# A hybrid decoder step on one core: ScalarE's and VectorE's order of work in the delta stage

## The chip, the cores and the metric

The kernel runs on one core of a Trainium2 chip. Its time is the device time of one execution in microseconds (us); several runs are given by their median. Engines carry the names of the profile: PE is TensorE (PEld its weight loads), DVE is VectorE, ACT is ScalarE, POOL is GpSimd, SP is SyncE, which here only issues transfers.

## What is computed

One layer of a decoder for 528 prompt tokens (16 learned ones and 512) and 8 sample sequences of 4 tokens, all float32. Cut to what matters:

```python
def gdn_chunk(S, q, k, v, g, beta):            # one chunk of tokens, 4 heads of 128
    G = jnp.cumsum(g, axis=-1)
    decay = jnp.exp(jnp.where(incl, G[..., :, None] - G[..., None, :], -jnp.inf))
    kb = k * beta[..., None]
    L = jnp.where(strict, jnp.einsum('bhik,bhjk->bhij', kb, k) * decay, 0.0)
    rhs = jnp.concatenate([v * beta[..., None], kb * jnp.exp(G)[..., None]], axis=-1)
    sol = lax.linalg.triangular_solve(L, rhs, left_side=True, lower=True, unit_diagonal=True)
    ...
    return S_new, o

def token_mixer(...):
    proj = xn @ w_in                           # q, k, v, z, a, b and the Conformer's input
    ...                                        # short convolution, l2norm of q and k
    S_new, o = gdn_prompt(S0f, q, k, v, g, beta) if prompt else gdn_recurrent(...)
    o = rmsnorm(o.transpose(0, 2, 1, 3), gdn_norm_w) * jax.nn.silu(z)
    c = causal_dwconv(c_ext, conf_dw_w) + conf_dw_b      # 31 taps, 512 channels
    c = jax.nn.silu(layernorm(c, conf_ln_w, conf_ln_b))
    out = jnp.concatenate([o, c], axis=-1) @ w_out
    return out, ...

h = h + token_mixer(rmsnorm(h)); h = h + peer_ffn(rmsnorm(h))   # then a last RMSNorm
```

`peer_ffn` picks 16 of 16384 one-neuron experts per head and token (8 heads) and adds their outputs up.

## The kernel before, in words

**Stages.** The span falls into the input projection, the delta stage (about 140 to 404 us: the chunks of the recurrence, the Conformer's convolution and layer norm, the last blocks of the input projection, the sample sequences), the output and query projections (404 to 530), the choice of experts, and two dense passes over all experts (to 1237 and to the end), each step of which PE computes while the next weights are split into a high and a low part.

**The delta stage.** The prompt is cut into chunks 0 (48 rows: 32 of the sample, 16 learned tokens) and 1 to 4 (128 rows each). Each engine has a generator `tile(ci)` for each chunk that yields named steps: `gb` (cumulated gates), `k` (keys transposed to rows), `khT` (normalized keys transposed back), `kk` and `kq` (products of keys, and of keys and queries), `ldT`, `v`, `p2` to `t3` (inverse of the 16-wide diagonal blocks), `n` to `nt4` and `r0` to `r3` (the solve), `wT`, `ws`, `qs`, `su`, `o1` (state and output). `ke` is ScalarE's step that scales the transposed keys into `RA` (second half) and `KE` (for chunk 0 `KEM`). Other generators run beside the chunks: `late_blocks` (20 units of the input projection, each two halves of 12 matmuls on PE and an evacuation on ScalarE), `sample_tile` (`sw0` to `sw3`, `ktm`, `su00` to `su31`), `norm_tile_conf` (layer norm: sums `ls`, squares `sq`, `lv`, root `lr`, inverse root `li`, products `lm` on VectorE, SiLU `ln` on ScalarE), `mix_tile` (`conformer`, `cl0` to `cl3`: high and low parts of the layer norm's output, `high`: high part of the first output weights, `table`, `delta`), `outs`, `roots`, `onbs` (RMSNorm of the recurrence's outputs: `oss` sums of squares, `root`, `onb`, `on`).

**What sets the order.** A table gives each step a time: `FIRST[ci]` plus `LEVEL[n]` or, for a few steps, `HEAD[n][ci]`; the other generators have tables of absolute times (`SAMPLE_AT`, `OUT_AT`, `NORM_AT`, `MIX_AT`). `side_by_side` (L507) writes out, for each engine by itself, always the generator whose next step has the lowest time. An engine then works strictly in this order; a wait of one step holds everything behind it. The same times deal out the PSUM banks: `GROUPS` is sorted by them, a step takes the next bank of the ring, and `free_bank` (L1005) makes PE wait until those that read the bank before are done. The bank of `k` is given back by VectorE's `k` and ScalarE's `ke` (L474). VectorE's `feed` (L2287) puts the 124 accumulations of the convolution (L1943, 528 columns) between the steps by the same times.

**Steps that the change touches**, before: ScalarE runs the exponentials of a chunk (L1533 to L1536, eight instructions) in step `gb`, at `HEAD["gb"]`, ahead of `ke` (L1541 and L1550) and `khT` (`take`, L1523: a copy out of PSUM). Chunk 3 alone has `khT` ahead of `ke`. VectorE's `kk` waits for the exponentials (L2086). The sums of squares of the outputs of the sample and chunks 1 and 2 are on ScalarE (L1611: four squares with an accumulated sum), those of chunks 3 and 4 on VectorE (L2168: a product of 512 columns, L2169: a reduction). The low part of the first output weights is GpSimd's (L848); it waits for ScalarE's `high`.

Of the kernel before, what the change touches and what calls it, by code (L numbers as in the profile page):

```python
# [32 lines left out]
HEADS, DH = 4, 128  # L33
# [16 lines left out]
CHUNKS = [(0, MIXED)] + [(MIXED + P * i, P) for i in range(SEQ // P)]  # L50
# [123 lines left out]
def build(nc, ins, outs, counts):  # L174
# [13 lines left out]
    with ctx:  # L188
# [229 lines left out]
        for b in range(nb):  # L418
# [4 lines left out]
        SAMPLE, TAILS, NORM, LIN, MIX = range(len(CHUNKS), len(CHUNKS) + 5)  # L423
        OUTS = (SAMPLE, 1, 2, 3, 4)
        SET = {0: 0, 1: 0, 2: 0, 3: 2, 4: 0}
        FIRST = {0: 4.2, 1: 12.5, 2: 27.9, 3: 41.3, 4: 43.6}
        HEAD = {"gb": {0: -2.4, 1: -2, 2: -2.4, 3: -1.2, 4: -1.28}, "k": {0: -1.3, 1: -0.8, 2: -0.7, 3: -0.2, 4: -0.8},
                "ke": {0: -0.9, 1: -0.1, 2: -0.3, 3: 1.05, 4: -0.4}, "su": {0: 9.1, 1: 14, 2: 14, 3: 14, 4: 14.15}}
        END_AT = 54.65

        LEVEL = {"khT": 1, "kk": 2, "kq": 2.1, "ldT": 3, "v": 3.1, "p2": 4, "pt2": 4.1,
# [5 lines left out]
        SAMPLE_AT = {"sw0": 42.4, "sw1": 42.9, "sw2": 43.7, "sw3": 44.2, "ws": 44.25, "qs": 44.3, "o1": 45.2}  # L437
        for hh in range(HEADS):
            SAMPLE_AT[f"ktm{hh}"] = 49.4 + 1.2 * hh
            SAMPLE_AT[f"su{hh}0"], SAMPLE_AT[f"su{hh}1"] = 50.2 + 1.2 * hh, 50.25 + 1.2 * hh  # L440
        OUT_AT = {"oss": {SAMPLE: 46.5, 1: 46.6, 2: 46.7, 3: 55.45, 4: 57.82},
                  "root": {SAMPLE: 46.8, 3: 56.65, 4: 58.02},
                  "onb": {SAMPLE: 48.9, 1: 50.1, 2: 51.1, 3: 56.68, 4: 58.05},
                  "on": {SAMPLE: 49.6, 1: 50.7, 2: 51.7, 3: 57.8, 4: 58.95}}
        NORM_AT = {"ls": 48.5, "lc": 48.55, "sq0": 49.3, "sq1": 49.35, "lv0": 50.3, "lv1": 50.8, "sq2": 50.85,
                   "lv2": 51.3, "sq3": 51.32, "lv3": 51.75, "lr": 51.85, "li0": 52.2, "li1": 52.45}
        for c in range(NG):
            NORM_AT[f"lm{c}"], NORM_AT[f"ln{c}"] = 52.5 + 0.2 * c, 52.6 + 0.2 * c
        MIX_AT = {"conformer": 53.8, "cl0": 54.0, "cl1": 54.2, "cl2": 54.4, "cl3": 54.6, "high": 54.8, "table": 55.65,
                  "out0a": 57.85, "out1a": 57.9, "out2a": 57.95, "delta": 57.96, "deltalow": 58, "out0b": 58.6,  # L450
                  "out1b": 58.9, "out2b": 59.2}
        TAILS_AT = {"tail0": 40.65, "tail1": 40.85, "tail2": 41.05, "tail3": 41.2}
# [888 lines left out]
        def _(act):  # L1341
            def fn(out, in_, f, *name, **kw):
                return A.op(act.activation(out, in_, f, **kw), *name)
# [167 lines left out]
            def each_head(n, out, in_, scale, ci):  # L1511

                for hh in range(HEADS):
                    fn(out(hh), in_(hh), ACT.Identity, *((n, ci) if hh == HEADS - 1 else ()), scale=scale(hh))

            def tile(ci):
                c0, c = CHUNKS[ci]
                B = SETS[SET[ci]]
                KH, KHT, KE, RA, RB, M, AT, VN = (B[n_] for n_ in ("KH", "KHT", "KE", "RA", "RB", "M", "AT", "VN"))
                if ci == 0:  # L1520
                    KE = KEM

# [8 lines left out]
                yield "gb", ci
                V.wait(act, "arg", ci)
                for hh in range(HEADS):  # L1533
                    fn(M[6][0:c, hh, 0:c], M[6][0:c, hh, 0:c], ACT.Exp, bias=row_of(GCB, c, ci, hh), scale=-1.0)
                    fn(M[5][0:c, hh, 0:c], M[5][0:c, hh, 0:c], ACT.Exp, "exp", ci, bias=row_of(NGC, c, ci, hh),
                       scale=1.0)  # L1536
                if ci == len(CHUNKS) - 2:
                    yield "khT", ci
                    take("khT", KHT[:, :, 0:c], P)
                    yield "ke", ci  # L1540
                    V.wait(act, "k", ci)  # L1541
                    if ci == 1:
                        T.wait(act, "r0b", 0)
                    if ci == 0:
                        V.wait(act, "qconv", 3 * HEADS - 1)
                    each_head(None, lambda hh: RA[0:c, hh, 1, :], of_head("k"), lambda hh: row_of(RKB, c, ci, hh), ci)
                    each_head("ke", lambda hh: KE[0:c, hh, :], of_head("k"), lambda hh: row_of(RKE, c, ci, hh), ci)
                else:
                    yield "ke", ci
                    V.wait(act, "k", ci)  # L1550
                    if ci == 1:
                        T.wait(act, "r0b", 0)
                    if ci == 0:
                        V.wait(act, "qconv", 3 * HEADS - 1)
                    each_head(None, lambda hh: RA[0:c, hh, 1, :], of_head("k"), lambda hh: row_of(RKB, c, ci, hh), ci)
                    each_head("ke", lambda hh: KE[0:c, hh, :], of_head("k"), lambda hh: row_of(RKE, c, ci, hh), ci)
# [259 lines left out]
        def _(dve):  # L1816
# [778 lines left out]
```

## Time and profile before

| | us |
|---|---|
| median of 3 runs | 1844.85 |
| lowest, highest run | 1838.57, 1849.69 |
| the profiled execution, its own time | 1842.69 |
| its span, first to last instruction | 1840.9 |
| PE busy in the span | 1777.0 (97%) |
| DVE busy | 1384.3 (75%) |
| ACT busy | 712.9 (39%) |
| POOL busy | 681.8 (37%) |
| mean granted clock of PE | 0.991 |

The profile is of one execution. Busy time is the time in which an engine executes; a timeline gives an instruction's start, its length and, in brackets, how long its engine sat idle before it and whose end ended that. PEclk is the TensorE clock that was granted, as a share of full speed. Plain float32 matmuls appear twice each (four of a step as x8), transposes and the split projections once.

### The profile page before, as it was taken

How to read it: one execution, taken by the hardware profiler on the slowest of the kernel's cores; microseconds unless marked ns; L12 is line 12 of the kernel's file. 1: busy time of each engine (PE TensorE's matmuls, PEld its weight loads, DVE VectorE, ACT ScalarE, POOL GpSimd, SP SyncE). 2: the span in 40 equal slices, each digit the busy share in tenths (PEclk: the TensorE clock that was granted, in tenths of full speed). 3: DMA queues.
4: the chain of work that ended last, by engine and by line, in shares of the span. 5: the costliest groups of instructions: out<-in, count | busy, mean ns of one | idle time of the engine just before them, and what ended most of it. 6: DMA issues, size and time to landing. Idle time of an engine off the chain costs nothing.

```text
span 1840.9 us, 29413 instructions
## 1 busy us (share of the span) xinstructions
PE 1777.0 (97%) x11497; PEld 1728.0 (94%) x11497; DVE 1384.3 (75%) x2533; ACT 712.9 (39%) x1244; POOL 681.8 (37%) x448
## 2 busy tenths in 40 slices
PE   7999987979999999999999999999999999999998
PEld 6998886879999999999999999999999999999997
DVE  4887887674899999999865665437697888887752
ACT  4546325453333334443433333333233333333332
POOL 3000000000004586777876767742353333333100
PEclk9999999999999999999999999999999999999999
DMA  7211101053313688888998989899999999999731
GB/s 215 69 47 43 36 5 49 24 150 124 118 47 111 218 275 264 295 294 311 300 322 293 308 313 318 289 378 354 338 402 374 339 347 361 342 342 355 293 118 38
DMA packets 190706, 424.33 MB, mean 231 GB/s; under 512 B 11162, under 2 KB 119222, under 8 KB 180320
## 3 DMA queue, kind: packets, MB, share of 16 engines
q1 hardware_dynamic: 153256, 287.47, 45.3%
q0 software_dynamic: 37312, 134.97, 20.8%
q8 instruction: 92, 1.51, 0.3%
q14 instruction: 46, 0.38, 0.1%
HBM read 360.76 MB, written 62.06 MB: 230 GB/s over the span
## 4 chain that ended last, share of the span: by engine, by line
PE 75%; DVE 19%; ACT 3%; issue 2%; POOL 1%; DMA 0%; SPq 0%; DVEq 0%; ACTq 0%; POOLq 0%
PE psum L1321 32%; PE psum L1300 21%; PE psum L927 9%; PE psum L1288 3%; PE psum L922 3%; DVE cT L1943 2%; DVE junk L2461 2%; PE psum L1030 2%; PE psum L1078 1%; DVE besti L2336 1%; DVE oh L2451 1%; DVE besti L2324 1%; DVE sring L2328 1%; DVE eqx L2394 1%; DVE pick L2399 1%
## 5 line engine op out<-in xcount | busy, mean ns | idle before, releaser
L1300 PE MATMUL psum<-xT,WS 128*128 128x416 f32 x3072 | 594.8, 353 | 2.8 <-POOL WS L862 2.7
L1321 PE MATMUL psum<-AR,WS 128*128 128x416 f32 x3072 | 582.1, 351 | 2.6 <-DVE AR L2532 2.6
L1321 PEld LDWEIGHTS psum<-AR,WS 128*128 128x128 f32 x3072 | 575.6, 188 | 9.0 <-DVE AR L2532 3.0
L1300 PEld LDWEIGHTS psum<-xT,WS 128*128 128x128 f32 x3072 | 572.2, 188 | 8.5 <-POOL WS L862 4.0
L862 POOL TENSOR_TENSOR WS<-RAWP,WS 128x1024 fp32r<-128x1024 f32 x128 | 310.9, 2439 | 315.6 <-ACT WS L1730 215.0
L853 POOL DMA_INDIRECT rowg<-in_expert_v,idx x128 | 182.0, 1422 | 317.6 <-DVE acc L2475 309.7
L927 PE MATMUL psum<-xT,WR 128*128 128x280 f32 (+2 forms) x1968 | 272.0, 296 | 4.7 <-DVE WR L1830 3.3
L1740 ACT ACTIVATE WS<-RAWP 128x1024 fp32r<-128x1024 f32 x128 | 135.6, 1059 | 336.2 <-PE psum L1321 325.9
L927 PEld LDWEIGHTS psum<-xT,WR 128*128 128x128 f32 x1968 | 258.1, 191 | 6.6 <-DVE WR L1830 3.6
L2525 DVE TENSOR_TENSOR WS<-RAWP,WS 128x1024 fp32r<-128x1024 f32 x128 | 156.5, 1223 | 116.2 <-ACT WS L1740 116.2
L1767 ACT ACTIVATE actA<-psum 128x416 f32<-128x416 f32 x128 | 66.3, 518 | 401.8 <-PE psum L1300 395.5
L2461 DVE CUSTOM_DVE_ANT_0 junk<-rowg,psum 128x1024 bf16<-128x1024 f32 x128 | 155.9, 1218 | 51.8 <-DMA rowg<-in_expert_u_rows,idx 43.8
L853 POOL DMA_INDIRECT rowg<-in_expert_u_rows,idx x128 | 166.0, 1297 | 37.6 <-issue 22.7
L2475 DVE SCALAR_TENSOR_TENSOR acc<-rowg,coef,acc 128x1024 f32<-128x1024 f32 x128 | 163.8, 1279 | 3.2 <-DMA rowg<-in_expert_v,idx 1.0
L2451 DVE TENSOR_TENSOR oh<-iotab,pairs 128x2048 bf16<-128x2048 bf16 x52 | 93.7, 1801 | 93.0 <-PE psum L1288 92.2
L1730 ACT ACTIVATE WS<-RAWP 128x1024 fp32r<-128x1024 f32 x128 | 134.5, 1053 | 0.0
L1943 DVE SCALAR_TENSOR_TENSOR cT<-gext,dwcols,cT 128x528 f32<-128x528 f32 x120 | 92.3, 769 | 4.2
L840 POOL MEMSET WQP<- 128x2048 f32 x1 | 1.8, 1809 | 246.9 <-PE psum L927 246.9
L2454 DVE TENSOR_TENSOR ohg<-oh,pairs 128x3072 bf16<-128x3072 bf16 x52 | 91.5, 1759 | 1.8
L2523 DVE TENSOR_TENSOR act<-act,Gt 128x416 f32<-128x416 f32 x128 | 74.9, 585 | 12.7 <-DMA act<-act_dram 9.1
L1792 ACT ACTIVATE AR<-act 128x416 fp32r<-128x416 f32 x128 | 69.0, 539 | 36.9 <-DVE act L2523 36.9
L2532 DVE TENSOR_TENSOR AR<-act,AR 128x416 fp32r<-128x416 f32 x128 | 74.9, 585 | 7.3 <-ACT AR L1792 7.3
(372 smaller groups left out, 1662.0 us busy)
## 6 DMA issues: line engine op xcount, KB each, us to landing
RAWP<-in_expert_u SPq DMA_DIRECT2D x64, 1024.0 KB
RAWP<-in_expert_v SPq DMA_DIRECT2D x64, 1024.0 KB
act_dram<-actA SPq DMA_DIRECT2D x128, 208.0 KB
gate_dram<-gblk SPq DMA_DIRECT2D x26, 1024.0 KB
act<-act_dram SPq DMA_DIRECT2D x64, 416.0 KB
Gt<-gate_dram SPq DMA_DIRECT2D x16, 1664.0 KB
RAW<-in_w_in SPq DMA_DIRECT2D x8, 1024.0 KB, 6.0
RAW<-in_w_query SPq DMA_DIRECT2D x8, 1024.0 KB, 8.0
```

The lines of the kernel that those rows point to most:

```text
L853: pool.indirect_dma_start(out=rowg[:, s_ % 4, :], out_offset=None, in_=table, in_offset=bass.IndirectOffsetOnAxis(ap=idx[:, s_ % PAIRS:s_ ...
L862: pool.tensor_tensor(ws(n)[:, 1], raw(n), ws(n)[:, 0].bitcast(F32), ALU.subtract).then_inc(u_low, 1)
L927: last = mm(bank[u % 4][:, 0:hw], W[:, pw, kt, m * P:(m + 1) * P], xT[:, px, kt, c0:c0 + hw], **go)
L1300: last = mm(bank[e % 2][:, 0:TD], ws(e)[:, pw, kt * P:(kt + 1) * P], xT[:, px, kt, TSP:TPE], start=(kt == 0 and i == 0), stop=(kt == KT - ...
L1321: last = mm(bank[dt][:, 0:TD], ws(NK + e)[:, pw, dt * P:(dt + 1) * P], AR[:, e % 4, pa, :], start=(e == 0 and i == 0), stop=(e == NK - 1 a ...
L1730: act.activation(ws(n)[:, 0], raw(n), ACT.Copy).then_inc(u_high, 1)
L1740: act.activation(ws(n)[:, 0], raw(n), ACT.Copy).then_inc(v_high, 1)
L1943: op(dve.scalar_tensor_tensor(d, x, w, d, ALU.mult, ALU.add))
L2451: chain(tt(by_two(oh[:, i]), keys_, per_token(0, 2), ALU.is_equal))
L2461: dve.tensor_tensor_reduce(junk[:], rowg[:, s_ % 4, :], xnP, 1.0, 0.0, ALU.mult, ALU.add, sdot[:, s_:s_ + 1]).then_inc(dot_done, 1)
L2475: dve.scalar_tensor_tensor(acc[:], rowg[:, s_ % 4, :], coef[:, s_:s_ + 1], acc[:], ALU.mult, ALU.add).then_inc(axpy_done, 1)
L2525: tt(ws(NK + e)[:, 1], raw(NK + e), ws(NK + e)[:, 0].bitcast(F32), ALU.subtract).then_inc(v_low, 1)
```

## The change

It does three things.

1. ScalarE's exponentials get a step of their own, `exp`, with a row of times of its own. For chunk 0 the order on ScalarE becomes `khT`, `exp`, `ke` (before: `gb`, `ke`, `khT`), at 5.2, 5.25 and 5.3 instead of 1.8, 3.3 and 5.2. For chunk 4 the step moves from 42.32 to 42.4, so that chunk 3's `ke` (42.35) comes first on ScalarE.
2. The layer norm's second inverse root, its products and its SiLU get later times (`li1` 52.45 to 52.87, `lm` 52.5 + 0.2c to 52.95 + 0.25c, `ln` 52.6 + 0.2c to 53.31 + 0.25c), the sample's `su20` and `su21` go from 52.6 and 52.65 to 52.92 and 52.94, `conformer` and `cl0` to `cl3` are moved too.
3. Chunk 3's sums of squares move from VectorE to ScalarE, to just ahead of `root`.

Nothing else is computed in another way, and no transfer is added or taken away.

By these times the orders become the following, where they differ (before, then after; the number behind the point is the chunk, S the sample):

```
ACT  unit0 gb.0 ke.0 unit1 khT.0 unit2 | unit0 unit1 khT.0 exp.0 ke.0 unit2
ACT  khT.3 gb.4 ke.3 ke.4              | khT.3 ke.3 exp.4 ke.4
ACT  n2.4 ln0 ln1 nt2.4 ktm3.S ln2 ln3 wT.3 nt4.4 | n2.4 nt2.4 ktm3.S wT.3 ln0 ln1 nt4.4 ln2 ln3
ACT  wT.4 table root.3                 | wT.4 table oss.3 root.3
PE   n2.4 su20 su21 r1a.4 r1b.4 nt2.4  | n2.4 r1a.4 r1b.4 nt2.4 su20 su21
DVE  li1 lm0 su20 su21 r1a.4 lm1 r1b.4 lm2 ktm3.S lm3 r2a.4 | r1a.4 r1b.4 li1 su20 su21 lm0 ktm3.S lm1 lm2 r2a.4 lm3
DVE  cl0 cl1 ws.3                      | cl0 ws.3 cl1
DVE  o1.3 oss.3 ws.4                   | o1.3 ws.4 oss.3
```

```diff
-        HEAD = {"gb": {0: -2.4, 1: -2, 2: -2.4, 3: -1.2, 4: -1.28}, ...
-                "ke": {0: -0.9, 1: -0.1, 2: -0.3, 3: 1.05, 4: -0.4}, ...
+        HEAD = {"gb": {0: -2.4, 1: -2, 2: -2.4, 3: -1.2, 4: -1.2},
+                "exp": {0: 1.05, 1: -2, 2: -2.4, 3: -1.2, 4: -1.2}, ...
+                "ke": {0: 1.1, 1: -0.1, 2: -0.3, 3: 1.05, 4: -0.4}, ...
+        SAMPLE_AT["su20"], SAMPLE_AT["su21"] = 52.92, 52.94
-        OUT_AT = {"oss": {SAMPLE: 46.5, 1: 46.6, 2: 46.7, 3: 55.45, 4: 57.82},
+        OUT_AT = {"oss": {SAMPLE: 46.5, 1: 46.6, 2: 46.7, 3: 56.62, 4: 57.82},
-                   "lv2": 51.3, "sq3": 51.32, "lv3": 51.75, "lr": 51.85, "li0": 52.2, "li1": 52.45}
+                   "lv2": 51.3, "sq3": 51.32, "lv3": 51.75, "lr": 51.85, "li0": 52.2, "li1": 52.87}
-            NORM_AT[f"lm{c}"], NORM_AT[f"ln{c}"] = 52.5 + 0.2 * c, 52.6 + 0.2 * c
-        MIX_AT = {"conformer": 53.8, "cl0": 54.0, "cl1": 54.2, "cl2": 54.4, "cl3": 54.6, ...
+            NORM_AT[f"lm{c}"], NORM_AT[f"ln{c}"] = 52.95 + 0.25 * c, 53.31 + 0.25 * c
+        MIX_AT = {"conformer": 54.1, "cl0": 54.2, "cl1": 54.35, "cl2": 54.5, "cl3": 54.65, ...
...
+                if ci == 0:
+                    yield "khT", ci
+                    take("khT", KHT[:, :, 0:c], P)
+                    yield "exp", ci
+                    exps()
+                    yield "ke", ci
+                    keys()
...
             def outs():
-                for i, ci in enumerate(OUTS[:-2]):
+                for i, ci in enumerate(OUTS[:-1]):
...
                     yield "oss", ci
-                    if ci in OUTS[-2:]:
+                    if ci == OUTS[-1]:
                         squares = SETS[SET[ci]]["RB"][:, :, 0, :]
```

`exps()` and `keys()` hold the instructions that stood in `gb` and `ke`, with the same waits. For chunks 1, 2 and 4 the order inside a chunk is `exp`, `ke`, `khT`, for chunk 3 `exp`, `khT`, `ke`, as before.

## Rows read from the trace of the kernel before

**Rows 1.** The page's part on the chain that ended last, by engine

```profile
PE 75%; DVE 19%; ACT 3%; issue 2%; POOL 1%; DMA 0%; SPq 0%; DVEq 0%; ACTq 0%; POOLq 0%
```

**Rows 2.** Busy time by stretch: start:end, length, each engine's busy (count), PEclk, DMA

```profile
404.00:530.00 126.00, 125.46 (x1041) 125.02 (x1039) 87.70 (x342) 44.12 (x77) 0.00 (x0) 1.00 0.33 102
...
295.00:300.00 5.00, 5.00 (x22) 4.34 (x22) 1.46 (x2) 2.17 (x8) 0.00 (x0) 0.50 0.00 0
```

**Rows 3.** The same view, the stretch in which chunk 0 starts

```profile
140.00:155.09 15.09, 11.96 (x100) 10.92 (x100) 6.61 (x14) 11.69 (x33) 0.00 (x0) 0.89 0.06 10
```

**Rows 4.** Timeline of ScalarE at chunk 0 (start, length, operation, idle before)

```profile
146.14 0.34 ACT L1343 ACTIVATE KHT<-psum 128x192 f32<-128x192 f32 x1
```

**Rows 5.** Timeline of TensorE at chunk 0

```profile
141.22 0.45 PE L1044 MATMUL psum<-ident,KH 48*128 48x48 f32 x4
...
146.53 0.88 PE L1047 MATMUL psum<-KHT 128*48 128x48 f32 x8 [3.13 <-ACT KHT L1343]
...
147.90 2.67 PE L927 MATMUL psum<-xT,WR 128*128 128x280 f32 x12
```

**Rows 6.** Timeline of ScalarE, exponentials of chunk 4 and keys of chunk 3

```profile
290.20 2.44 ACT L1343 ACTIVATE M<-M,tok 128x128 f32<-128x128 f32 x8 [3.55 <-DVE M L2082]
...
293.55 1.13 ACT L1343 ACTIVATE KE<-psum,tok 128x128 f32<-128x128 f32 x4
```

**Rows 7.** Timeline of TensorE behind them

```profile
286.84 1.96 PE L1140 MATMUL psum<-SS,WQP 128*64 128x128 f32 x16
...
294.82 1.09 PE L1042 MATMUL psum<-ident,kC 128*128 128x128 f32 x4 [6.03 <-ACT KE L1343]
...
295.84 3.68 PE L1140 MATMUL psum<-SS,WQP 128*64 128x128 f32 x16
...
305.33 0.66 PE L1053 MATMUL psum<-ident,M 128*128 128x128 f32 x4
```

**Rows 8.** Busy time of the same stretch

```profile
290.20:305.44 15.24, 10.62 (x69) 9.70 (x70) 6.45 (x10) 6.65 (x24) 0.00 (x0) 0.78 0.26 68
```

**Rows 9.** The view of tile SS: its loads, time from issue to landing

```profile
L641 SPq DMA_DIRECT2D SS<-in_state_gdn x4: 368/458/581, 274.0 to 289.4; - x4
...
DMA to landing us min/median/max: 4.0/4.6/5.3
```

**Rows 10.** Timeline of TensorE behind the norm products

```profile
373.87 2.04 PE L1030 MATMUL psum<-M,M 128*128 128x128 f32 x8 [4.89 <-ACT M L1343]
```

**Rows 11.** Busy time from the first reciprocal of the norm to chunk 3's squares

```profile
363.77:388.30 24.53, 18.44 (x112) 16.15 (x112) 20.79 (x32) 14.81 (x28) 2.08 (x1) 0.86 0.28 79
```

**Rows 12.** Timeline of VectorE at the end of the stage

```profile
385.66 0.68 DVE L2250 TENSOR_TENSOR xT<-cT,xT 128x512 fp32r<-128x512 f32 x1
...
388.30 3.00 DVE L2168 TENSOR_TENSOR RB<-vC 128x512 f32<-128x512 f32 x1
...
392.45 0.69 DVE L2138 TENSOR_TENSOR VN<-RA,psum 128x512 f32<-128x512 f32 x1
...
398.04 0.69 DVE L2168 TENSOR_TENSOR RB<-vC 128x512 f32<-128x512 f32 x1
```

**Rows 13.** Timeline of ScalarE at the end of the stage

```profile
378.60 2.39 ACT L1343 ACTIVATE xT<-cT 128x128 fp32r<-128x128 f32 x5
...
384.18 1.90 ACT L1343 ACTIVATE WR<-RAW 128x2048 fp32r<-128x2048 f32 x1
...
388.37 1.28 ACT L1343 ACT_TABLE_LOAD   x1
...
394.64 1.26 ACT L1343 ACTIVATE state<-state,tok 128x128 f32<-128x128 f32 x4
```

**Rows 14.** Timeline of ScalarE: squares of chunk 1, first and last of eight rows

```profile
315.49 0.31 ACT L1343 ACTIVATE RB<-vC 128x128 f32<-128x128 f32 x1
...
316.58 0.19 ACT L1343 ACTIVATION_READ_ACCUMULATOR RB<-vC 128x1 f32 x1
```

**Rows 15.** Timeline of GpSimd in the delta stage

```profile
386.22 4.53 POOL L848 TENSOR_TENSOR WR<-RAW,WR 128x2048 fp32r<-128x2048 f32 x1 [108.20 <-ACT WR L1343]
```

More of the change, by code:

```diff
@@ L426, in build @@
         FIRST = {0: 4.2, 1: 12.5, 2: 27.9, 3: 41.3, 4: 43.6}
-        HEAD = {"gb": {0: -2.4, 1: -2, 2: -2.4, 3: -1.2, 4: -1.28}, "k": {0: -1.3, 1: -0.8, 2: -0.7, 3: -0.2, 4: -0.8},
-                "ke": {0: -0.9, 1: -0.1, 2: -0.3, 3: 1.05, 4: -0.4}, "su": {0: 9.1, 1: 14, 2: 14, 3: 14, 4: 14.15}}
+        HEAD = {"gb": {0: -2.4, 1: -2, 2: -2.4, 3: -1.2, 4: -1.2},
+                "exp": {0: 1.05, 1: -2, 2: -2.4, 3: -1.2, 4: -1.2}, "k": {0: -1.3, 1: -0.8, 2: -0.7, 3: -0.2, 4: -0.8},
+                "ke": {0: 1.1, 1: -0.1, 2: -0.3, 3: 1.05, 4: -0.4}, "su": {0: 9.1, 1: 14, 2: 14, 3: 14, 4: 14.15}}
         END_AT = 54.65
@@ L445, in build @@
         NORM_AT = {"ls": 48.5, "lc": 48.55, "sq0": 49.3, "sq1": 49.35, "lv0": 50.3, "lv1": 50.8, "sq2": 50.85,
-                   "lv2": 51.3, "sq3": 51.32, "lv3": 51.75, "lr": 51.85, "li0": 52.2, "li1": 52.45}
+                   "lv2": 51.3, "sq3": 51.32, "lv3": 51.75, "lr": 51.85, "li0": 52.2, "li1": 52.87}
         for c in range(NG):
-            NORM_AT[f"lm{c}"], NORM_AT[f"ln{c}"] = 52.5 + 0.2 * c, 52.6 + 0.2 * c
-        MIX_AT = {"conformer": 53.8, "cl0": 54.0, "cl1": 54.2, "cl2": 54.4, "cl3": 54.6, "high": 54.8, "table": 55.65,
+            NORM_AT[f"lm{c}"], NORM_AT[f"ln{c}"] = 52.95 + 0.25 * c, 53.31 + 0.25 * c
+        MIX_AT = {"conformer": 54.1, "cl0": 54.2, "cl1": 54.35, "cl2": 54.5, "cl3": 54.65, "high": 54.8, "table": 55.65,
                   "out0a": 57.85, "out1a": 57.9, "out2a": 57.95, "delta": 57.96, "deltalow": 58, "out0b": 58.6,
@@ L1529, in of_head, with exps, keys @@
                     return lambda hh: gbank(n, ci)[0:c, hh * P:(hh + 1) * P]
[L1531 to L1540, printed above, removed]
+                def exps():
+                    V.wait(act, "arg", ci)
+                    for hh in range(HEADS):
+                        fn(M[6][0:c, hh, 0:c], M[6][0:c, hh, 0:c], ACT.Exp, bias=row_of(GCB, c, ci, hh), scale=-1.0)
+                        fn(M[5][0:c, hh, 0:c], M[5][0:c, hh, 0:c], ACT.Exp, "exp", ci, bias=row_of(NGC, c, ci, hh),
+                           scale=1.0)
+                def keys():
                     V.wait(act, "k", ci)
@@ L1547, in tile @@
                     each_head("ke", lambda hh: KE[0:c, hh, :], of_head("k"), lambda hh: row_of(RKE, c, ci, hh), ci)
-                else:
+                if ci == 0:
[5 more added lines that the diff above has]
+                    keys()
+                elif ci == len(CHUNKS) - 2:
+                    yield "exp", ci
+                    exps()
+                    yield "khT", ci
+                    take("khT", KHT[:, :, 0:c], P)
+                    yield "ke", ci
+                    keys()
+                else:
+                    yield "exp", ci
+                    exps()
                     yield "ke", ci
[L1550 to L1556, printed above, removed]
+                    keys()
                     yield "khT", ci
```

## The prediction

> **What bounds the kernel now.** I read the page's chain first: three quarters of what ended last is PE's, a fifth DVE's [rows 1]. Then the stretches: from 404 us to 530 us PE is busy all but 0.5 us, and the two expert passes are of that kind, so what the delta stage (about 140 to 404 us) ends earlier, everything behind it starts earlier; nothing there catches it up. Inside the delta stage neither engine is full, and the reader is to see PE standing still and then running at half its clock, 1.2 of 2.4 GHz, as it does from 295 us to 300 us [rows 2]. So the change is worth what it takes from the waits that end last in that stage. I then read the timelines of PE, ACT and DVE side by side at each of the places that the change reorders, and compared the order tables, engine by engine.
>
> **Chunk 0: keys ahead of the exponentials.** PE has transposed the normalized keys at 141.67 us, but ScalarE copies them out at 146.14 us only, behind the table load, the eight exponentials and the two groups of keys; PE does one more half unit and waits 3.13 us [rows 4, 5]. Behind that wait a half unit of 12 matmuls takes 2.67 us instead of some 1.8. With the copy first PE goes on at about 143.2 us. The next limit is ScalarE's own queue: from 140.00 us to 155.09 us it is busy 11.69 us of 15.09 [rows 3], so 3.40 us of waiting for PE can go; in their place come some 0.65 us, in which it waits for unit 1 and for the transposes (141.22 to 141.67 us [rows 5], where before it had work from 140.7 us on). The work and the number of table loads are the same. Gain 3.40 - 0.65 = **2.7 us**. Bounds: 0 if VectorE, which waits for the exponentials, has to make up its work behind 160 us anyway, and 4.3 if PE's 3.13 us and its slow half unit both come back. Moved past unit 1's evacuation nothing waits for the exponentials but `kk.0` on VectorE, and that comes earlier too, since PE does. I take the middle value since the convolution's pieces lie at fixed places of the order and aren't made more.
>
> **Chunk 4's exponentials behind chunk 3's keys.** PE's transpose `k.4` needs the bank that ScalarE's `ke.3` gives back. ScalarE is idle for 3.55 us, from 286.65 us on, waiting for VectorE with chunk 4's exponentials in front; those take 2.44 us, and `ke.3` ends at 294.68 us. PE stands 6.03 us, then runs `k.4` in 1.09 us and the sixteen L1140 matmuls in 3.68 us, where the same sixteen took 1.96 us before the wait [rows 6, 7]. With `ke.3` first it runs in that idle time: 286.65 + 2.1 = 288.8 us, just when `sw0` ends on PE. Then `k.4` 0.6, `sw1` 2.0, `kk` and `kq` 2.0 give 293.4 us; `sw2` and `sw3` 3.7 to 4.0 end at 297.4 us, and `ldT.3` follows there, against 305.33 us [rows 7]. Gain 305.3 - 297.4 = **7.9 us**. Two things could hold it up. VectorE: it has 6.45 us of work in that stretch [rows 8], and 7.2 us are left for it, just enough. The loads of the third and fourth state, issued by 289.4 us, land after 4.0 to 5.3 us [rows 9], so by 294.7 us, in time for `sw3` and at most half a us late for `sw2`. The exponentials themselves run when they did, at 290.20 us, and `ke.4` behind them waits for nothing new. Bounds: 6.0 (the wait alone) to 8.5.
>
> **The norm products behind the solves.** ScalarE's copy `nt2.4` stands behind the SiLU `ln0`, `ln1`, and these behind VectorE's products. PE, which needs it for `nt4.4`, waits 4.89 us and comes out at the slow clock (2.04 us for a product of 1.05) [rows 10]. After the change `nt2.4` is copied as soon as it is there, about 366.7 us, and PE reaches `nt4.4` at about 369.0 us, held now by `wT.3`. That isn't the gain, for VectorE then sets the pace: between the first reciprocal and chunk 3's squares it is busy 20.79 us of 24.53 [rows 11]. The 3.74 us of idle can go but for the small gaps between dependent instructions; all its operands arrive earlier than it does. `su30` waits for `ktm3` on PE, but VectorE comes to it only 2 us later. Gain **3.1 us**, bounds 0 and 3.7.
>
> **Chunk 3's squares to ScalarE.** On VectorE they cost 388.30 to 392.42 us: 3.00 us for the product, then a reduction and two small ones; the same product for chunk 4 takes 0.69 us [rows 12]. The first ran beside GpSimd's subtraction, 386.22 to 390.75 us [rows 15], and ended 0.55 us after it. Products of that time with an operand in PSUM weren't slowed. The Trainium skill (SBUF — State Buffer, Who interferes with whom) has for this that VectorE with two inputs in SBUF and a reading GpSimd take one port pair by turns, whichever is second waiting for the whole of the first; the trace agrees (3.00 against 0.69). On ScalarE the squares come behind the table load (388.37 to 389.65 us) and a small root [rows 13], at 1.6 us past `o1.3`; four squares with their sums are 1.28 us [rows 14], and two small VectorE steps 0.35. That is 3.3 us past `o1.3` against 4.1. `ws.4` (0.69 us at 392.45 [rows 12]) no longer lies between the root and what follows: 0.4 us more. Chunk 4's decay of the state, which ends this chain at 395.90 us [rows 13], is thus **1.3 us** earlier. Squares behind a square-root table need no load of their own: none stands between the others of this stage and that table, and I take none here; if one did it would be 1.3 us, and this part nothing. Bounds 0 and 2.5.
>
> **Sum.** 2.7 + 7.9 + 3.1 + 1.3 = 15.0 us. The profiled execution took 1842.69 us, so 1827.7; it lies 2.2 us below the median of the runs, and for the median I say 1844.85 - 15.0 = 1829.8 us. The bounds added up are 6.0 and 19.0. A difference over 0.5%, 9.2 us, is about what a measurement of this kernel can tell from none.
>
> **Rivals.**
>
> *GpSimd gets in front of `cl3`.* The low parts `cl0` to `cl3` have both inputs in SBUF. Before, `cl3` began at 385.66 us [rows 12] and GpSimd at 386.22, 0.56 us later, because ScalarE had waited for PE; now both start from the last norm product. VectorE needs some nine steps of about 0.63 us and a small one until `cl3`, 5.9 us; ScalarE needs SiLU 0.8, the high parts 2.39, the decay 1.2 and the weights' high part 1.90 [rows 13], with the hand-over 6.5 us. The margin is 0.6 us. If VectorE loses it, `cl3` waits for GpSimd to end, which by rows 12 and 15 puts it some 4.8 us late, and the chain behind it as well: 15.0 - 4.8 = 10.2 us, a median of 1834.6. For it speaks the thin margin, against it that `cl2` and `cl3` have little in front that can be late. Chance 0.22. The rule of the Trainium skill (SBUF — State Buffer, Who interferes with whom) that the second to issue waits for the whole of the first would give the same.
>
> *One of the first two gains is absorbed.* VectorE is the fuller engine of the two hundred us between chunk 0 and chunk 3, and in the second place it has only 0.7 us to spare; were 8 us lost, by convolution pieces that cannot be fitted in, the gain is 7 us, a median of 1838. Chance 0.13.
>
> *The change doesn't do what it says*: a bank or an order elsewhere in the chain keeps the old pace and nothing comes of it, within 3 us of 1844.85. Against it, I find no new wait in the bank table: `k.4` still follows `k.3`, and the moved `su20` and `su21` take over banks freed by VectorE earlier. Chance 0.05.
>
> *Slower, by TensorE's clock.* Where PE stood for 5 us it ran at 0.50 of the granted clock for the next 5 [rows 2], and the same work took 1.9 times as long [rows 7]. If the new order brought such a fall into the dense stretch behind 404 us, where the clock is 1.00, each us at the low level would cost 0.47 us. It takes 32 us of it to eat the gain and 52 us to make the kernel slower by 9.2, a median of 1854. Nothing in the rows shows a fall without PE idle ahead of it, and the change takes such idle time away. Chance 0.03.
>
> The forecast has 0.57.
>
> **How the numbers follow.** The likeliest time is 1829.8. With the median's own scatter of some 3 us it spans 1825 to 1834; the range goes down to 1823 for the upper bounds and up to 1840 for the second rival, leaving out the last two and the tails. Faster by over 0.5%: nearly all of the forecast's 0.57 less 0.04 for scatter, 0.6 of the first rival, a fifth of the second: 0.53 + 0.13 + 0.03 = 0.69. Slower: 0.03. The rest, 0.28, is within 0.5%.
>
> **What would show it.** After chunk 0's `khT` PE goes on without the 3.13 us, and the half unit behind takes 1.8 us. `k.4` starts within 1 us of `sw0`'s end, and the L1140 groups take 1.96 us each. `nt4.4` follows `wT.3` at once. VectorE is busy over nine tenths from the first reciprocal to `o1.3`, L2168 is there once, and the ACT chain load, four squares, root, scaling, decay sets the last state update. Wrong would be: `cl3` at 3 us or more beside GpSimd's subtraction (the first rival); a PE wait for a load at `sw2`; VectorE full between 290 and 310 us with PE waiting for it; a table load ahead of the new squares.

## The result, and the profile after

The changed kernel takes 1825.2 us (median of 7 runs, 1819.19 to 1831.03), the kernel before 1844.58 us (7 runs, 1838.57 to 1849.69). The ratio is 0.9895, with an interval of 0.9874 to 0.9916: faster by 1%. A second set of runs of the same two kernels gave 0.9907 (0.988 to 0.9934); one execution of each in that set, at a granted clock of 0.75, took 2189.97 and 2202.12 us and isn't counted. The prediction was 1829.8 us in a range of 1823 to 1840, with a chance of 0.69 on faster.

The profiled execution of after took 1819.19 us, its span is 1817.5 us and its mean granted clock 0.994, against 1842.69, 1840.9 and 0.991. The chain by engine, to be held against [rows 1]:

```profile
PE 73%; DVE 18%; ACT 3%; issue 2%; DMA 2%; POOL 1%; SPq 0%; DVEq 0%; ACTq 0%; POOLq 0%
```

The shares are nearly those of before. They say that no new engine has become the bound, and nothing of where 23 us went. For that I cut the execution at marks that both traces have on PE: `gb.0` (the cumulated gates of chunk 0), `sw0` (the first L1142 group of sixteen), `ldT.3`, the first reciprocal of the norm on VectorE (`li0`), `out0b` (the second half of the first output projection, which needs the low parts of the recurrence's outputs), and the start of the last expert pass. In us:

| part | before | after | less by |
|---|---|---|---|
| start to `gb.0` | 135.47 | 134.37 | 1.10 |
| `gb.0` to `sw0` (chunk 0's keys) | 151.37 | 148.62 | 2.75 |
| `sw0` to `ldT.3` (chunk 4's exponentials) | 18.49 | 10.09 | 8.40 |
| `ldT.3` to `li0` | 58.44 | 58.70 | -0.26 |
| `li0` to the end of `o1.3` (norm products) | 24.50 | 20.97 | 3.53 |
| `o1.3` to `out0b` (squares) | 12.30 | 11.16 | 1.14 |
| `out0b` to the last expert pass | 837.11 | 837.15 | -0.04 |
| last expert pass | 582.08 | 575.22 | 6.86 |

The delta stage, `gb.0` to `out0b`, went from 265.10 to 249.54 us: 15.6 us, where the prediction's sum is 15.0. Two parts that the change doesn't touch, the start and the last pass, gave another 8 us in this pair of executions; between the medians (19.4 us) only some 4 us are left beside the stage. Both parts are taken up below.

The stretches of after, with the columns of [rows 2]: the whole stage; chunk 0's start; from the `k.4` transposes to `ldT.3`; from the first reciprocal to VectorE's `ws.4`, the first step behind `o1.3`; and the dense stretch behind the stage.

```profile
134.37:383.91 249.54, 224.06 (x1666) 208.06 (x1665) 197.68 (x321) 128.67 (x334) 8.03 (x10) 0.97 0.17 45
140.00:151.00 11.00, 9.22 (x90) 8.24 (x89) 4.99 (x13) 10.34 (x27) 0.00 (x0) 1.00 0.01 2
285.00:293.10 8.10, 8.08 (x69) 7.47 (x69) 7.67 (x12) 4.49 (x16) 0.00 (x0) 1.00 0.51 129
351.78:374.83 23.05, 19.38 (x122) 17.55 (x121) 20.61 (x32) 16.90 (x33) 4.10 (x1) 0.89 0.42 105
388.00:514.00 126.00, 125.46 (x1040) 125.02 (x1039) 87.73 (x347) 44.48 (x78) 0.00 (x0) 1.00 0.33 102
```

Each stretch shows what is full now. At chunk 0 it is ScalarE, 10.34 of 11.00 us (before 11.69 of 15.09 [rows 3], which holds six instructions more: 33 against 27). Ahead of `ldT.3` it is PE and VectorE both, 8.08 and 7.67 of 8.10 us, at a clock of 1.00 (before 0.78 [rows 8]). Behind the first reciprocal VectorE works 20.61 us, the same work as before (20.79 [rows 11]), and all of it in the 20.97 us up to the end of `o1.3` (before 24.50). Behind the stage PE is busy all but 0.54 of 126 us, as in [rows 2]: nothing there could give the gain back.

The places themselves, on PE's timeline of after (start, length, idle before in brackets). The first group of `KHT` is chunk 0's, the one at 285.02 us is `k.4`, the one at 356.51 us `wT.3` and the last `nt4.4`.

```profile
140.50 1.81 PE L929 MATMUL psum<-xT,WR 128*128 128x280 f32 x12
142.23 0.56 PE L1049 MATMUL psum<-KHT 128*48 128x48 f32 x8
...
143.09 1.81 PE L929 MATMUL psum<-xT,WR 128*128 128x280 f32 x12
...
285.02 0.63 PE L1044 MATMUL psum<-ident,kC 128*128 128x128 f32 x4
285.57 1.96 PE L1142 MATMUL psum<-SS,WQP 128*64 128x128 f32 x16
...
293.08 0.66 PE L1055 MATMUL psum<-ident,M 128*128 128x128 f32 x4
...
356.51 0.66 PE L1108 MATMUL psum<-ident,RA 128*128 128x128 f32 x4
357.00 1.06 PE L1032 MATMUL psum<-M,M 128*128 128x128 f32 x8
```

The product of `KHT` follows the half unit at once, where [rows 5] has 3.13 us in front of it, and the half unit behind takes 1.81 us instead of 2.67. The `k.4` transposes begin 2 us behind the start of `sw0` and take 0.63 us instead of 1.09; the L1142 groups behind them run at 1.96 us instead of 3.68 [rows 7]. `nt4.4` follows `wT.3` (356.51 us) without a wait and takes 1.06 instead of 2.04 us [rows 10].

ScalarE at chunk 0 has one wait left, ahead of the copy that now comes first:

```profile
140.60 0.33 ACT L1345 ACTIVATE KHT<-psum 128x192 f32<-128x192 f32 x1 [0.68 <-PE psum L1046]
```

The end of the stage on ScalarE, to be held against [rows 13]:

```profile
372.85 1.28 ACT L1345 ACT_TABLE_LOAD   x1
374.14 0.20 ACT L1345 ACTIVATE tok<-tok 128x4 f32<-128x4 f32 x1
374.44 0.31 ACT L1345 ACTIVATE RB<-vC 128x128 f32<-128x128 f32 x1
...
375.53 0.19 ACT L1345 ACTIVATION_READ_ACCUMULATOR RB<-vC 128x1 f32 x1
376.15 0.20 ACT L1345 ACTIVATE tok<-tok 128x4 f32<-128x4 f32 x1 [0.43 <-DVE tok L2184]
376.80 1.28 ACT L1345 ACTIVATE ONB<-vC,tok 128x128 f32<-128x128 f32 x4 [0.44 <-DVE tok L2192]
377.98 1.26 ACT L1345 ACTIVATE state<-state,tok 128x128 f32<-128x128 f32 x4
```

Load, small root, four squares with their sums, root, scaling, decay, with no second table load: the chain that was predicted. The decay ends at 379.24 us, 6.49 us past `o1.3`, where it was 7.63 (395.90 against 388.27). On VectorE and GpSimd, `cl3` (the first row) and GpSimd's subtraction:

```profile
370.14 0.68 DVE L2261 TENSOR_TENSOR xT<-cT,xT 128x512 fp32r<-128x512 f32 x1
370.74 0.68 DVE L2146 TENSOR_TENSOR RA<-RB,psum 128x512 f32<-128x512 f32 x1
...
374.83 0.69 DVE L2149 TENSOR_TENSOR VN<-RA,psum 128x512 f32<-128x512 f32 x1 [2.09 <-PE psum L1112]
```

```profile
370.73 4.53 POOL L850 TENSOR_TENSOR WR<-RAW,WR 128x2048 fp32r<-128x2048 f32 x1 [96.54 <-ACT WR L1345]
```

`cl3` began 0.59 us ahead of GpSimd; the prediction had 0.6. So its first rival failed by the margin that it named. The second row is `r3b.4`, the solve's last step on VectorE: PE's `wT.4`, and behind it PE's part of `ws.4`, wait for it.

### The profile page after: what moved, and what is told of

The parts are those of the page before. It is cut to its first block, busy times and chain, and to the rows that moved or that the text cites. A ratio compares the mean times of both kernels' runs of the same rounds, so it can differ in the third digit from the quotient of the medians.

```text
span 1817.5 us, 29420 instructions
## 1 busy us (share of the span) xinstructions
PE 1766.2 (97%) x11497; PEld 1721.6 (95%) x11497; DVE 1382.2 (76%) x2531; ACT 714.2 (39%) x1252; POOL 682.8 (38%) x448
## 4 chain that ended last, share of the span: by engine, by line
PE 73%; DVE 18%; ACT 3%; issue 2%; DMA 2%; POOL 1%; SPq 0%; DVEq 0%; ACTq 0%; POOLq 0%
PE psum L1323 30%; PE psum L1302 21%; PE psum L929 10%; PE psum L1290 3%; PE psum L924 3%; DVE cT L1954 2%; DVE junk L2472 2%; DMA act<-act_dram 2%; PE psum L1032 2%; PE psum L1080 1%; DVE oh L2462 1%; DVE besti L2347 1%; DVE besti L2335 1%; DVE sring L2339 1%; DVE eqx L2405 1%
## 5 line engine op out<-in xcount | busy, mean ns | idle before, releaser
L1323 PE MATMUL psum<-AR,WS 128*128 128x416 f32 x3072 | 574.0, 348 | 3.9 <-DVE AR L2543 3.9
```

Source lines behind the costliest of these rows:

```text
L1323: last = mm(bank[dt][:, 0:TD], ws(NK + e)[:, pw, dt * P:(dt + 1) * P], AR[:, e % 4, pa, :], start=(e == 0 and i == 0), stop=(e == NK - 1 a ...
```

## The experiments

Nine kernels in ten runs. The first four each undo one part; then come two executions again, the one large part put into the kernel before by itself, two variants at the end of the stage, and the comparison again in five rounds. The profiled executions, by the marks of above (us; the fourth column of marks is `li0` to `out0b`):

| kernel | time | `gb.0` to `sw0` | to `ldT.3` | to `li0` | to `out0b` | stage |
|---|---|---|---|---|---|---|
| before | 1842.69 | 151.37 | 18.49 | 58.44 | 36.80 | 265.10 |
| before, again | 1842.12 | 151.41 | 18.47 | 58.44 | 36.79 | 265.11 |
| after | 1819.19 | 148.62 | 10.09 | 58.70 | 32.13 | 249.54 |
| after, again | 1828.00 | 148.50 | 10.19 | 59.71 | 32.65 | 251.05 |
| without part 1 (chunk 0) | 1837.07 | 153.99 | 10.08 | 60.92 | 32.64 | 257.63 |
| the same, again | 1829.44 | 151.46 | 10.09 | 58.73 | 32.13 | 252.41 |
| without chunk 4's move | 1836.01 | 148.56 | 18.24 | 58.46 | 32.67 | 257.93 |
| without the norm part | 1830.89 | 148.55 | 10.09 | 58.71 | 35.65 | 253.00 |
| without the squares | 1830.70 | 148.61 | 10.08 | 58.74 | 33.29 | 250.72 |
| before with chunk 4's move | 1838.45 | 151.55 | 10.10 | 58.73 | 36.79 | 257.17 |
| after with a late `cl3` | 1836.19 | 150.05 | 10.80 | 59.73 | 34.58 | 255.16 |
| after with an earlier table load | 1836.98 | 148.57 | 10.10 | 58.84 | 31.72 | 249.23 |

One execution's whole time is a poor witness: those with a stage of 250.72 and 253.00 us took 1830.70 and 1830.89. The parts repeat to 0.1 or 0.2 us in most columns, so I read them. The last two columns do so less: after and its repeat differ by 1.0 us in `ldT.3` to `li0` and by 0.5 us in the last one.

**Chunk 0's order undone** (ScalarE: `exp.0`, `ke.0` ahead of `khT.0` again).

```diff
-                "exp": {0: 1.05, 1: -2, ...
-                "ke": {0: 1.1, 1: -0.1, ...
+                "exp": {0: -2.4, 1: -2, ...
+                "ke": {0: -0.9, 1: -0.1, ...
...
-                if ci == 0:
-                    yield "khT", ci
-                    take("khT", KHT[:, :, 0:c], P)
-                    yield "exp", ci
-                    exps()
-                    yield "ke", ci
-                    keys()
-                elif ci == len(CHUNKS) - 2:
+                if ci == len(CHUNKS) - 2:
```

> The changed kernel with chunk 0 back in its old order on ScalarE (exponentials, keys, then the copy khT). Measure: the delta stage, from the start of PE's gb.0 to the start of the first-output matmuls out0b; it is 265.1 us in the profile of the kernel before (135.47 to 400.57) and 249.5 us in that of the changed one (134.37 to 383.91). Theory (the places add up): PE's wait of some 3.1 us behind khT returns and the stage is 2.8 us longer, 252.3 us. Rival (VectorE makes up its work behind 160 us anyway): 249.5 to 250.5 us.

Measured: a stage of 257.63 us, 8.1 more than in after, where 2.8 were expected. PE's timeline has the wait back, and behind it a half unit slower than in before:

```profile
148.43 0.87 PE L1049 MATMUL psum<-KHT 128*48 128x48 f32 x8 [3.13 <-ACT KHT L1345]
...
149.80 3.17 PE L929 MATMUL psum<-xT,WR 128*128 128x280 f32 x12
```

The excess lies mostly in two columns, and in the second of them, `ldT.3` to `li0`, nothing was edited. Either this part is worth three times the 2.7 us, or the clock fell differently in this execution. So I ran the same kernel again.

> The same kernel as no_chunk0, for a second profile. The first had the stage 8.1 us longer than the changed kernel (257.6 us) instead of 2.8 us, with the slow clock in places where the other profiles have none. Theory (the places add up, the rest was chance of the clock): 252.3 us. Rival (chunk 0's order is worth 8 us, through the clock behind its wait): 257 us or more again.

Measured: 252.41 us, 2.9 above after, and 2.8 of it in the column `gb.0` to `sw0`. The same wait of 3.13 us, and no slow half unit behind it:

```profile
147.82 0.56 PE L1049 MATMUL psum<-KHT 128*48 128x48 f32 x8 [3.13 <-ACT KHT L1345]
...
148.68 1.80 PE L929 MATMUL psum<-xT,WR 128*128 128x280 f32 x12
```

The part is worth 2.8 us. This agrees with every other row of the table but two: the column reads 151.4 to 151.6 with the old order (before twice, the repeat here, before with chunk 4's move) and 148.5 to 148.6 with the new one in six executions. In the two that stand out, 153.99 and 150.05, the granted clock of the column is 0.96 and 0.98, against 0.98 in the repeat of the one and 0.99 in after. The excess isn't the edits': the repeat of the first doesn't have it, and the late `cl3` lies 200 us behind the column.

Before has the slow half unit (2.67 us) in this column and the repeat has not (1.80 us), and the columns are 151.37 and 151.46 us. So the slow half unit cost nothing that reaches `sw0`.

**Chunk 4's exponentials ahead of chunk 3's keys again.**

```diff
-                "exp": {0: 1.05, ..., 4: -1.2}, ...
+                "exp": {0: 1.05, ..., 4: -1.28}, ...
```

> The changed kernel with chunk 4's exponentials back ahead of chunk 3's keys on ScalarE. Theory: PE waits about 6.0 us ahead of k.4, runs sw1 at half the clock, and the stage is 8.4 us longer, 257.9 us. Rival (only the wait counts, the slow clock is hidden behind VectorE): 6.0 us longer, 255.5 us.

Measured: 257.93 us against the 257.9 expected, but not all of these 8.4 us are the edit's. The edited column is 8.15 us longer (18.24 against 10.09), the next one 0.24 shorter, and the last one, where nothing was edited, 0.54 longer, which after's own repeat shows too (0.52). That leaves 7.9 us, and the exact hit is in part luck. The rival's 6.0 us are clearly passed. PE's timeline is that of [rows 7] again, wait and slow group to the last digit:

```profile
292.50 1.09 PE L1044 MATMUL psum<-ident,kC 128*128 128x128 f32 x4 [6.03 <-ACT KE L1345]
293.52 3.68 PE L1142 MATMUL psum<-SS,WQP 128*64 128x128 f32 x16
```

**The same move alone, in the kernel before**, asks whether the parts lean on each other.

```diff
-        HEAD = {"gb": {0: -2.4, ..., 4: -1.28}, ...
+        HEAD = {"gb": {0: -2.4, ..., 4: -1.2}, ...
```

> The kernel before with one number changed: chunk 4's step gb at -1.2 instead of -1.28, so that chunk 3's keys are scaled ahead of chunk 4's exponentials. Theory (it stands alone): the stage is 8.4 us shorter than before, 256.7 us. Rival (it needs the other parts): 1 to 6 us shorter, 259 us or more.

Measured: 257.17 us, half a us more than expected. `sw0` to `ldT.3` took 10.10 us against 18.49, 8.4 us less, as in the whole change; but `ldT.3` to `li0` took 0.29 us more (58.73 against 58.44). Every execution with the move shows at least 58.70 there, and the three without it 58.44 to 58.46: the move gives back 0.3 us, and its net worth is 8.1 us. It needs none of the other parts. One number of one row makes half of the stage's gain.

**The norm part undone.**

```diff
-        SAMPLE_AT["su20"], SAMPLE_AT["su21"] = 52.92, 52.94
...
-                   "lv2": 51.3, ..., "li1": 52.87}
+                   "lv2": 51.3, ..., "li1": 52.45}
-            NORM_AT[f"lm{c}"], NORM_AT[f"ln{c}"] = 52.95 + 0.25 * c, 53.31 + 0.25 * c
-        MIX_AT = {"conformer": 54.1, "cl0": 54.2, "cl1": 54.35, "cl2": 54.5, "cl3": 54.65, ...
+            NORM_AT[f"lm{c}"], NORM_AT[f"ln{c}"] = 52.5 + 0.2 * c, 52.6 + 0.2 * c
+        MIX_AT = {"conformer": 53.8, "cl0": 54.0, "cl1": 54.2, "cl2": 54.4, "cl3": 54.6, ...
```

> The changed kernel with the old times of the layer norm, of su20 and su21 and of the high and low parts (conformer, cl0 to cl3). Theory: VectorE's 3.5 us of idle time return, with PE's wait of 4.9 us ahead of nt4.4, and the stage is 3.5 us longer, 253.0 us. Rival (the gain of 3.5 us came with the squares' move, since GpSimd's subtraction now starts earlier): under 1.5 us longer.

Measured: 253.00 us, all of the 3.5 in the last column, and PE waits as in [rows 10]:

```profile
364.79 2.04 PE L1031 MATMUL psum<-M,M 128*128 128x128 f32 x8 [4.89 <-ACT M L1344]
```

**Chunk 3's squares back on VectorE.**

```diff
-        OUT_AT = {"oss": {..., 3: 56.62, 4: 57.82},
+        OUT_AT = {"oss": {..., 3: 55.45, 4: 57.82},
-                for i, ci in enumerate(OUTS[:-1]):
+                for i, ci in enumerate(OUTS[:-2]):
-                    if ci == OUTS[-1]:
+                    if ci in OUTS[-2:]:
```

> The changed kernel with chunk 3's sums of squares back on VectorE, ahead of ws.4. Theory: the product L2179 starts 2.0 us behind GpSimd's subtraction again and lasts about 3.0 us instead of 0.69; the stage is 1.1 us longer, 250.7 us. Rival (the slow product had another cause than GpSimd): it lasts 0.7 us and the stage is 249.5 us or shorter.

Measured: 250.72 us, 1.2 more than after. The product has its 3 us again, VectorE's timeline and then GpSimd's:

```profile
376.42 3.02 DVE L2179 TENSOR_TENSOR RB<-vC 128x512 f32<-128x512 f32 x1
379.48 0.69 DVE L2180 TENSOR_REDUCE tok<-RB 128x4 f32<-128x512 f32 x1
```

```profile
374.37 4.52 POOL L850 TENSOR_TENSOR WR<-RAW,WR 128x2048 fp32r<-128x2048 f32 x1 [96.59 <-ACT WR L1345]
```

It ends at 379.44 us, 0.55 behind GpSimd's end (378.89), the same 0.55 as in [rows 12, 15]. The four undone parts sum to 2.9 + 8.4 + 3.5 + 1.2 = 16.0 us, or 15.5 with chunk 4's 7.9, against 15.6 for all together: they add up.

**The kernel before again**, to know how far two executions of one kernel differ in the stage.

> The kernel before, unchanged, for a second profile. Theory (the difference of 6.9 us in the last dense pass between the two first profiles, 582.08 and 575.22 us, is of the execution and not of the kernel): stage 265.1 us, and the pass takes either of the two lengths. Rival (it belongs to the kernel): 582.1 us again; this one profile can only refute it.

Measured: 265.11 against 265.10 us. The last column's 36.79 and the first's 151.41 repeat too. So before repeated where the undone kernel and the changed one did not; with two executions of each, no more is said by that. The last expert pass took 582.10 us, the same length again, so this profile refutes neither side.

**`cl3` late.** The first rival said what would happen if VectorE lost the 0.6 us. This moves `cl3` alone, so that it comes second, though at another place of VectorE's order: behind `r3b.4` and `su.3` and no longer ahead of them.

```diff
-        MIX_AT = {..., "cl3": 54.65, ...
+        MIX_AT = {..., "cl3": 55.35, ...
```

> The changed kernel with cl3, a subtraction with both inputs in SBUF, behind VectorE's su.3 instead of ahead of r3b.4, so that it starts some 0.6 us behind GpSimd's subtraction. Theory (VectorE waits for the end of GpSimd's instruction): it lasts about 4.4 us instead of 0.69, o1.3 ends 3.7 us later and the stage is some 2.1 us longer, 251.6 us. Rival (only the product of the squares was slow): it lasts 0.7 us and the stage is 249.5 us.

Measured: the stage took 255.16 us, but 3.2 of the 5.6 us above after fell ahead of `li0`, where nothing is edited. Behind `li0` it took 34.58 us against 32.13, so 2.45 us (1.9 against the 32.65 of after's repeat), where 2.1 were expected. `cl3` itself took 4.04 us where 4.4 were expected. Timelines of VectorE, of PE at `wT.4` and of GpSimd:

```profile
376.96 0.69 DVE L2155 TENSOR_TENSOR state<-state,psum 128x512 f32<-128x512 f32 x1 [0.27 <-PE psum L1116]
377.57 4.04 DVE L2261 TENSOR_TENSOR xT<-cT,xT 128x512 fp32r<-128x512 f32 x1
381.64 0.69 DVE L2158 TENSOR_TENSOR vC<-vC,psum 128x512 f32<-128x512 f32 x1
382.36 0.69 DVE L2149 TENSOR_TENSOR VN<-RA,psum 128x512 f32<-128x512 f32 x1
```

```profile
377.59 0.60 PE L1108 MATMUL psum<-ident,RA 128*128 128x128 f32 x4
```

```profile
376.54 4.52 POOL L850 TENSOR_TENSOR WR<-RAW,WR 128x2048 fp32r<-128x2048 f32 x1 [98.62 <-ACT WR L1345]
```

`cl3` ends 24.36 us behind `li0`, where it ended 19.04 us behind it in after: 5.3 us late by itself. The wait for GpSimd that the rival named was there. At this place it cost about half of its length: VectorE had 2.09 us of waiting for PE ahead of `ws.4` (374.83 us in after), and that took up a part of the lateness, since PE began `wT.4` (377.59 us) as `cl3` began. A step that is late costs less than its lateness where the engine waits later on anyway. The rival's own price of 4.8 us isn't tested by this. In its case `r3b.4` stands behind `cl3`, PE's `wT.4` and `ws.4` wait for `r3b.4`, and so VectorE's later wait would come late too and take up nothing.

**The table load earlier.** In after the load stands in the chain between the solve's last copy and the squares. This puts it, and the small root that goes with it in step `table`, ahead of the copy; the squares come right behind it, and with chunk 3's `root` and `onb` they are now ahead of `ws.4`.

```diff
-        OUT_AT = {"oss": {..., 3: 56.62, ...}, "root": {..., 3: 56.65, ...}, "onb": {..., 3: 56.68, ...
+        OUT_AT = {"oss": {..., 3: 56.55, ...}, "root": {..., 3: 56.57, ...}, "onb": {..., 3: 56.58, ...
-        MIX_AT = {..., "table": 55.65, ...
+        MIX_AT = {..., "table": 55.55, ...
```

> The changed kernel with the load of the square-root table ahead of chunk 4's wT copy on ScalarE, where it is idle for 1.7 us, and chunk 3's oss, root and onb ahead of ws.4. Theory (the chain load, squares, root, scaling, decay sets the stage's end): squares start as o1.3 ends, the decay ends 1.7 us earlier and the stage is about 248 us. Rival (ws.4, which waits for PE until 2.1 us past o1.3, holds the chain up at once): 249.0 to 249.5 us.

Measured in five rounds: 1827.7 us (1824.18 to 1836.98), a ratio to before of 0.9904 (0.9881 to 0.9927), no better than after. In its trace the last state decay ends 26.82 us behind `li0` instead of 27.46, 0.6 us sooner, and the long block of the projection (348 matmuls) starts 35.59 us behind `li0` instead of 36.01: 0.4 us. PE no longer waits at `out0b`, the 37th matmul of its group, which starts at 386.80 us; the stage is 249.23 us, where 248 was expected: the rival's range of 249.0 to 249.5. It held for a reason near its own. `ws.4`, now behind the small steps of the root on VectorE, comes 24.37 us behind `li0` instead of 23.05. The squares began 1.5 us earlier, and 0.9 us of that went to a product of four elements a partition:

```profile
377.52 1.05 DVE L2183 TENSOR_TENSOR tok<-tok 128x4 f32<-128x4 f32 x1 [1.50 <-ACT RB L1345]
```

It takes 0.16 us otherwise. Both its inputs are in SBUF, and GpSimd's subtraction ran from 374.02 to 378.55 us: the product ended 0.02 us behind it.

**After and before again, in five rounds.**

> The changed kernel once more, timed in five rounds against the one before and with a second profile. Theory (the stage gives 15.6 us, the rest of the 19.4 us between the first medians is scatter of the start, of the clock and of the pace in the last pass): stage 249 to 252 us, ratio 0.989 to 0.993. Rival (the change also makes the last pass faster, by 3 to 7 us on average): the last pass takes 575 us again, ratio 0.987 to 0.989.

Measured: after 1823.23 to 1830.23 us, before 1837.44 to 1848.64, ratio 0.9907 (0.988 to 0.9934). The profiled execution has a stage of 251.05 us and a last expert pass of 582.06 us. This was the run to tell whether the change had made the last pass shorter, as the first pair of traces suggests (575.22 against 582.08). It had not: here the changed kernel has the length of before.

## Why the prediction held

The waits that it named were the ones that went, at the places and in about the sizes that it gave. By its own steps, predicted and measured in us:

| step | predicted | bounds | measured |
|---|---|---|---|
| chunk 0, keys first | 2.7 | 0 to 4.3 | 2.8 |
| chunk 4's exponentials behind | 7.9 | 6.0 to 8.5 | 7.9 to 8.1 |
| norm products behind the solves | 3.1 | 0 to 3.7 | 3.5 |
| squares on ScalarE | 1.3 | 0 to 2.5 | 1.1 to 1.2 |
| sum | 15.0 | 6.0 to 19.0 | 15.6 |

**Chunk 0.** The step counted ScalarE's idle time, not PE's wait, since ScalarE was the engine that would be full next. It kept 0.65 us of idle time, and 0.68 us stood. The upper bound counted the slow half unit (2.67 us) besides; with it and without it the column is the same length, so nothing of it could be won.

**Chunk 4's exponentials.** The step named every wait that could come next, and none came: no load is waited for at `sw2`, and VectorE's work fitted. It was the closest call, VectorE being busy 7.67 of 8.10 us in front of `ldT.3`. The stretch from `sw0` took 10.09 us where the step had 10.56: it allowed up to 4.0 us for `sw2` and `sw3`, which took 3.71, and 4.6 for what lies ahead of them, which took 4.4. So the step itself gave 8.4 us, and the 0.3 us that the next stretch gave back was in no term.

**The norm products.** The step said that the wait of 4.89 us is not the gain, since VectorE sets the pace. It kept 0.6 us of its 3.74 us of idle time for gaps between dependent instructions; 0.36 us stood (20.97 less 20.61), and the work itself was 0.2 us less.

**The squares.** 1.1 us in the trace and 1.2 in the experiment, against 1.3. The wait for GpSimd that it escapes is shown by [rows 12, 15], by the kernel without this part, and by the late `cl3`. The rule cited ahead (Trainium skill, SBUF — State Buffer, Who interferes with whom) agrees with each of them: VectorE came second and ended 0.55 us behind GpSimd, while the products with an operand in PSUM beside it kept their 0.69 us.

**The rivals.** GpSimd in front of `cl3` didn't happen, by 0.59 us in after and 0.82 in its repeat. A `cl3` forced behind GpSimd at a later place cost 1.9 to 2.45 us; the 4.8 us for its own place stay an estimate that no run shows. The absorbed gain didn't happen: the four parts add up, less 0.3 us. The change did what it says. The clock in the dense stretch behind the stage stayed at 1.00.

**The median.** The prediction said 1829.8 us; 1825.2 was measured, and 1827.5 for the five runs of the repeat. The stage's 15.6 us leave 1844.58 - 15.6 = 1829.0, so 3.8 us of the first medians' difference are not the stage's, and the forecast of the median is closer to what the stage gave than to what was measured. Scatter can account for it: the first ratio's interval is a gain of 15.5 to 23.2 us, the second's 12.2 to 22.2, and 15.6 lies in both, in the first just so. Whether the changed kernel has the shorter last pass more often stays open; single profiles can't tell how often, and the one repeated had the long one.

## What to carry to other kernels

In a stage where no engine is full, take the engine that would be full next, count its idle time up to the next dependence, and call that the gain; the length of the wait in front of you is neither that gain nor a bound of it: here it was off by 1.4 us one way (4.89 for 3.5) and 2.1 us the other (6.03 for 8.1, as PE had lost its clock behind it). Where two engines start from one event and the loser waits for a whole operation, work out the margin before trusting the order, and ask what stands behind the late step: a later wait softens the loss only if it doesn't hang on that step. Before a single execution is used to price a part, run it twice and compare by marks in the trace: the whole time differed by 7.6 us between two executions of one kernel, and the marks put 5.2 of them into the delta stage, where the granted clock was lower in one (0.96 against 0.98 and 0.92 against 0.94 in its two long columns).

## What the runs showed of the hardware

**TensorE's clock falls at other places in executions of the same kernel.** The two executions without part 1 have the same order of work and the same wait of 3.13 us; behind it the same twelve matmuls took 3.17 us in one and 1.80 in the other. The granted clock of the two stretches, the first execution's and then the repeat's, is 0.50 and 1.00, so 1.2 and 2.4 GHz:

```profile
149.80:152.97 3.17, 3.17 (x15) 2.90 (x14) 0.28 (x1) 0.29 (x1) 0.00 (x0) 0.50 0.00 0
```

```profile
148.68:150.48 1.80, 1.80 (x17) 1.65 (x15) 0.38 (x2) 0.79 (x2) 0.00 (x0) 1.00 0.00 0
```

The half unit is 1.4 us of it; over the whole stage it was 257.63 against 252.41 us. After and its repeat differ by 1.5 us, before and its repeat by 0.01. No row that I read tells ahead which it will be.

**The last expert pass has two paces with the clock at 1.00.** Here is the same stretch of it, in before and then in after:

```profile
1528.70:1577.20 48.50, 48.50 (x258) 48.01 (x258) 39.70 (x47) 16.85 (x22) 19.55 (x14) 1.00 0.91 334
```

```profile
1512.10:1560.60 48.50, 48.50 (x262) 48.28 (x261) 39.53 (x47) 16.75 (x22) 19.47 (x14) 1.00 0.93 339
```

In 48.50 us PE did 258 matmuls, or 262. The records of the chain give 186.8 ns a matmul for the faster (475.15 us for 2544, in after) and 189.0 for the slower (480.80 for 2544, in the repeat without part 1). A pace holds until PE has to wait. The kernel without the norm part changed from the slow one to the fast one at the wait for the activations reloaded from DRAM, shown by its chain and by the stretches ahead of and behind that wait:

```profile
1229.37 65.30 PE psum L1322 x336
1298.80 30.53 DMA act<-act_dram
1332.83 475.15 PE psum L1322 x2544
```

```profile
1240.00:1285.00 45.00, 45.00 (x240) 44.54 (x239) 34.78 (x40) 15.14 (x20) 12.72 (x11) 1.00 0.92 342
1340.00:1385.00 45.00, 45.00 (x243) 44.84 (x242) 41.99 (x49) 17.52 (x23) 26.18 (x15) 1.00 1.01 406
```

The repeat without part 1 went the other way at the same wait (63.01 us for the 336, then 480.80). Before and after's repeat show a granted clock of 0.96 in the pass's first 48 us, and both took 582.1 us; after shows 1.00 there and took 575.22. Of the twelve profiled executions seven took 582.06 to 582.10 us; the others took 575.22, 578.62 (without the norm part), 580.19 (the repeat without part 1), 584.35 (before with chunk 4's move) and 590.12 (the earlier table load). In all twelve the pass began at the slower pace where the clock of its first 48 us was 0.94 to 0.96, ten times, and at the faster one where it was 1.00, twice. What sets the pace isn't shown. It is worth 7 us, almost half of this change's effect, and would have been booked to the change from one pair of profiles.

**The stage's start** lies between 134.37 and 138.00 us in the profiled executions, at the same code ahead of it. This alone is a fifth of the effect.
